# Summing part of the prompt's expert rows with ScalarE and the Pool, in a fused diffusion backbone step

## The reference, cut to what matters

```python
gate = jax.nn.softmax(best_s, axis=-1).astype(hb.dtype)
act = jax.nn.gelu(jnp.einsum('thkd,td->thk', u_tab[idx], hb), approximate=False)
return jnp.einsum('thk,thkd->td', gate * act, v_tab[idx])
...
x = x + g2 * peer_ffn(hff, lp['peer_wq'], lp['peer_keys'], lp['peer_u'], lp['peer_v'])
```

## Time and profile before

| | us |
|---|---|
| median of 3 runs | 4969.91 (4968.59 to 4973.04) |
| the profiled execution | 4967.69 |
| its span, first to last instruction | 4965.9 |
| TensorE (PE) matmuls busy | 3861.3 (78%) |
| VectorE (DVE) busy | 3242.6 (65%) |
| ScalarE (ACT) busy | 748.0 (15%) |
| Pool busy | 1447.9 (29%) |
| slot matmuls, line 680, in three groups by source | 1865.1 + 687.8 |
| dots, line 1218 | 831.5 + 420.8 + 312.1 |
| gathers, share of the 16 DMA engines | 67.4% |
| mean granted TensorE clock | 0.929 |

### The profile page before, as it was taken

How to read it: one execution, slowest core, us unless ns; L and a number is a source line. 1 busy time by engine, 2 the same in 40 slices (tenths; PEclk the granted TensorE clock), 3 DMA queues, 4 the chain that set the end, 5 groups by cost and what they waited for, 6 DMA issues and landing times. The chain is left out here.

```text
span 4965.9 us, 36487 instructions
## 1 busy us (share of the span) xinstructions
PE 3861.3 (78%) x11046; PEld 1898.0 (38%) x11046; DVE 3242.6 (65%) x8263; ACT 748.0 (15%) x2211; POOL 1447.9 (29%) x1284
## 2 busy tenths in 40 slices
PE   7588678988777776788868786788977687777776
PEld 6464334643222222235535443346422222222222
DVE  1546765536887868854574766664378787687666
ACT  0111124211101010010121112341010100100101
POOL 0001112212454434432222021221044354354432
PEclk9788788999999999999989897899999999999999
DMA  8334456754998999999969254566389899899998
GB/s 266 99 116 178 153 188 242 252 194 192 412 415 368 421 374 414 421 390 387 365 245 366 97 203 146 206 253 220 127 354 421 365 419 421 362 421 421 407 421 341
DMA packets 342149, 1497.72 MB, mean 302 GB/s; under 512 B 31424, under 2 KB 176448, under 8 KB 178112
## 3 DMA queue, kind: packets, MB, share of 16 engines
q0 software_dynamic: 184320, 1342.26, 67.4%
q1 hardware_dynamic: 157632, 153.13, 9.6%
HBM read 1491.97 MB, written 3.31 MB: 301 GB/s over the span
## 5 line engine op out<-in xcount | busy, mean ns | idle before, releaser
L680 PE MATMUL expert_acc<-uv_ring,diag 128*128 128x512 f32 x3744 | 1865.1, 631 | 417.9 <-DVE diag L1227 407.8
L634 POOL DMA_INDIRECT uv_ring<-uv,expert_index x936 | 1050.2, 1122 | 2717.1 <-PE expert_acc L680 2174.4
L680 PEld LDWEIGHTS expert_acc<-uv_ring,diag 128*128 128x128 f32 x3744 | 688.1, 198 | 1487.8 <-DVE diag L1227 898.5
L1218 DVE CUSTOM_DVE_ANT_0 uv_ring<-uv_ring,arena 128x1024 f32<-128x1024 f32 x680 | 831.5, 1223 | 243.2 <-DMA uv_ring<-uv,expert_index 240.5
L680 PE MATMUL expert_acc<-arena,diag 128*128 128x512 f32 x1376 | 687.8, 632 | 264.2 <-DVE diag L1227 196.3
L951 ACT ACTIVATE gelu<-u_dot 128x1 f32<-128x1 f32 x1280 | 256.0, 203 | 2943.8 <-DVE u_dot L1218 2943.2
L1227 DVE TENSOR_SCALAR diag<-const_mats,expert_gate,gelu 128x128 f32<-128x128 f32 x1280 | 465.7, 364 | 308.8 <-ACT gelu L951 214.1
L634 POOL DMA_INDIRECT arena<-uv,expert_index x344 | 397.6, 1156 | 757.2 <-PE expert_acc L680 460.3
L1218 DVE CUSTOM_DVE_ANT_0 arena<-arena 128x1024 f32<-128x1024 f32 x344 | 420.8, 1223 | 172.6 <-DMA arena<-uv,expert_index 171.2
L680 PEld LDWEIGHTS expert_acc<-arena,diag 128*128 128x128 f32 x1376 | 243.4, 195 | 698.1 <-DVE diag L1227 425.2
L1218 DVE CUSTOM_DVE_ANT_0 uv_ring<-uv_ring,prompt_rows 128x1024 f32<-128x1024 f32 x256 | 312.1, 1219 | 113.4 <-DMA uv_ring<-uv,expert_index 112.9
(11 more groups left out here) (202 smaller groups left out, 2785.0 us busy)
## 6 DMA issues: line engine op xcount, KB each, us to landing
w_ring<-w_ada SPq DMA_DIRECT2D x66, 512.0 KB, 11.3
w_ring<-w_in SPq DMA_DIRECT2D x64, 512.0 KB, 5.0
w_ring<-w_pq SPq DMA_DIRECT2D x64, 512.0 KB, 4.5
w_ring<-w_out SPq DMA_DIRECT2D x32, 512.0 KB, 6.3
uv_ring<-w_ada SPq DMA_DIRECT2D x30, 512.0 KB, 5.3
uv_ring<-uv,expert_index POOLq DMA_INDIRECT x936, 11.7
arena<-b_ada SPq DMA_DIRECT2D x48, 128.0 KB, 6.2
arena<-uv,expert_index POOLq DMA_INDIRECT x344, 15.7
```

The lines of the kernel that those rows point to most:

```text
L634: pool.indirect_dma_start(out=UV[j], out_offset=None, in_=uv, in_offset=bass.IndirectOffsetOnAxis(ap=idxs[:, n % 2, k:k + 1], axis=0)).the ...
L680: ins = pe.matmul(acc[:, half, :], diag[:, m % DIAGS, :], UV[SLOT_AT[m]][:, D + 512 * half:D + 512 * half + 512], start=(k == 0), stop=(k ...
L1218: V_.tensor_tensor_reduce(UV[j][:, 0:D], UV[j][:, 0:D], rows_of(n), 1.0, 0.0, ALU.mult, ALU.add, dots[:, m % DOTS:m % DOTS + 1]).then_inc( ...
```

## The change

In blocks 0 and 5, slots 84 to 127 take another path. VectorE's dot and ScalarE's gelu stay. ScalarE then multiplies gate and gelu (128x1) and multiplies the gathered v by it in place (128x1024). The Pool clears a 1024-column tile once per block and adds each weighted row to it, in its own queue between the gathers: before it issues the gather that reuses a buffer, it adds the row that lies there. VectorE builds no diag and TensorE issues no matmuls for these 44 slots. At m = 130 TensorE waits for the Pool's last add and adds its sum to `expert_acc` with two matmuls by the identity (`fold`); add_peer waits for that.

The table's rows change too: attention's steps advance by 1 each (24, m = 60 to 83), the output stage's by 2 and 1 in turn (24, m = 84 to 107), the second norm's by 3 as before, the sixteen query tiles by 1 each (m = 111 to 126). Four advances (m = 127 to 130) are left for `rest()`.

The diff, cut to its core; left out are the new buffer and semaphores, and four places where a wait for all sums of a block becomes `all_summed`:

```diff
@@ -142,7 +142,7 @@
 BESIDE_SAMPLE = points(("n1", [7], 2), ("pa", range(4), 2), ("pa", range(4, 8), 1), ("px", range(6), 1),
                        ("pg", range(4), 1), ("conv", [5], 4), ("taps", range(4, 30, 5), 2), ("cT", [3], 4), ("st", range(8), 3), ("yT", [3], 3), ("v", [4], 3), 
-                       ("head", range(0, 24, 2), 2), ("head", range(1, 24, 2), 1), ("wo", range(16), 1), ("n2", [7], 3), ("pq", range(8), 2))
+                       ("head", range(24), 1), ("wo", range(0, 16, 2), 2), ("wo", range(1, 16, 2), 1), ("n2", [7], 3), ("pq", range(16), 1))
 BESIDE_PROMPT = points(("mod", range(24), 2), ("n1", [1], 3), ("pa", range(2), 2), ("pz", range(2), 2), ("px", range(6), 1),
                        ("pg", range(4), 1), ("conv", [5], 2), ("taps", range(4, 30, 5), 1), ("cT", [0], 2), ("st", range(2), 3),
@@ -172,6 +172,29 @@
 SLOT_AT, SLOT_BEFORE, SLOT_TURN = slot_buffers()
+POOL_FROM = 84
+def by_pool(n, k):
+    return n % NBLK == 0 and k >= POOL_FROM
+def sums_before(n, k):
+    slots = [by_pool(m // SLOTS, m % SLOTS) for m in range(n * SLOTS + k)]
+    return slots.count(False), slots.count(True)
+PE_SLOTS = [m for m in range(L * NBLK * SLOTS) if not by_pool(m // SLOTS, m % SLOTS)]
+POOL_SLOTS = [m for m in range(L * NBLK * SLOTS) if by_pool(m // SLOTS, m % SLOTS)]
+TURN = {m: i for of in (PE_SLOTS, POOL_SLOTS) for i, m in enumerate(of)}
+FOLD_AFTER = {n: SLOTS + 2 for n in range(L * NBLK) if any(by_pool(n, k) for k in range(SLOTS))}
+FOLDS = sorted(FOLD_AFTER)
 class Beside:
...
@@ -426,6 +450,10 @@
         gsum = at(13568, 2, PH)
         htok = [at(13584, D), at(ARENA - 512 - D, D)]
         psum_out = at(ARENA - 512, 512)
+        def pool_sum(n):
+            return htok[1] if n % NBLK == 0 else htok_p[:]
         w_loaded = [ctx.enter_context(nc.semaphore(f"w_loaded{k}")) for k in range(NW + AHEAD)]
...
@@ -500,6 +531,20 @@
         def blk(l, g, b):
             return l * NBLK + FIRST_BLOCK[g] + b
+        def summed(eng, m):
+            if by_pool(m // SLOTS, m % SLOTS):
+                eng.wait_ge(s_pa, TURN[m] + 1)
+            else:
+                eng.wait_ge(s_vs, TURN[m] + 1)
+        def all_summed(eng, n):
+            pe_slots, pool_slots = sums_before(n, 0)
+            eng.wait_ge(s_vs, pe_slots)
+            if pool_slots:
+                eng.wait_ge(s_pa, pool_slots)
         def w_unit(l, g, kind, u):
...
@@ -616,13 +661,33 @@
         @block.gpsimd
         def _(pool):
+            def add_row(m, first):
+                n = m // SLOTS
+                if first:
+                    if n % NBLK == 0:
+                        pool.wait_ge(*s_sup.at(n // NBLK, 1, 7))
+                    else:
+                        pool.wait_ge(s_pup.sem, n)
+                    nc.gpsimd.memset(pool_sum(n), 0.0).then_inc(pool_chain, 1)
+                    pool.wait_ge(pool_chain, FOLDS.index(n) + 1)
+                else:
+                    pool.wait_ge(s_pa, TURN[m])
+                pool.wait_ge(s_pw, TURN[m] + 1)
+                nc.gpsimd.tensor_tensor(pool_sum(n), UV[SLOT_AT[m]][:, D:2 * D], pool_sum(n), ALU.add).then_inc(s_pa, 1)
             for l in range(L):
                 for g in range(2):
                     for b in range(GROUP_BLOCKS[g]):
                         n = blk(l, g, b)
+                        mine = [n * SLOTS + k for k in range(SLOTS) if by_pool(n, k)]
+                        added = 0
                         for k in range(SLOTS):
                             m = n * SLOTS + k
                             j = SLOT_AT[m]
+                            while added < len(mine) and mine[added] <= SLOT_BEFORE[m]:
+                                add_row(mine[added], added == 0)
+                                added += 1
                             if k == 0:
                                 pool.wait_ge(*s_idx.at(l, g, 2 * b))
                                 if g:
@@ -630,9 +695,11 @@
                             elif g and k == SLOTS // 2:
                                 pool.wait_ge(*s_idx.at(l, g, 2 * b + 1))
                             if SLOT_BEFORE[m] >= 0:
-                                pool.wait_ge(s_vs, SLOT_BEFORE[m] + 1)
+                                summed(pool, SLOT_BEFORE[m])
                             pool.indirect_dma_start(out=UV[j], out_offset=None, in_=uv,
                                                     in_offset=bass.IndirectOffsetOnAxis(ap=idxs[:, n % 2, k:k + 1], axis=0)).then_inc(s_gat[j], 16)
+                        for i in range(added, len(mine)):
+                            add_row(mine[i], i == 0)
         @block.tensor
@@ -675,15 +742,25 @@
                 m = n * SLOTS + k
                 if n and k == 0:
                     pe.wait_ge(s_pup.sem, n)
-                pe.wait_ge(s_dg, m + 1)
+                pe.wait_ge(s_dg, TURN[m] + 1)
                 for half in range(2):
-                    ins = pe.matmul(acc[:, half, :], diag[:, m % DIAGS, :], UV[SLOT_AT[m]][:, D + 512 * half:D + 512 * half + 512],
+                    ins = pe.matmul(acc[:, half, :], diag[:, TURN[m] % DIAGS, :], UV[SLOT_AT[m]][:, D + 512 * half:D + 512 * half + 512],
                                     start=(k == 0), stop=(k == SLOTS - 1), skip_group_check=True)
                 ins.then_inc(s_vs, 1)
+            def fold(n):
+                pe.wait_ge(s_pa, sums_before(n + 1, 0)[1])
+                for half in range(2):
+                    ins = pe.matmul(acc[:, half, :], C[:, C_ID, :], pool_sum(n)[:, 512 * half:512 * half + 512],
+                                    start=False, stop=(FOLD_AFTER[n] > SLOTS), skip_group_check=True)
+                ins.then_inc(s_fold, 1)
             def add_beside(n, m):
-                if 2 <= m <= SLOTS + 1:
+                if 2 <= m <= SLOTS + 1 and not by_pool(n, m - 2):
                     add_v(n, m - 2)
+                if m == FOLD_AFTER.get(n):
+                    fold(n)
             beside = Beside(add_beside)
@@ -950,9 +1027,20 @@
                 act.wait_ge(s_dot, m + 1)
                 nc.scalar.activation(gel[:, m % DOTS:m % DOTS + 1], dots[:, m % DOTS:m % DOTS + 1], ACT.Gelu).then_inc(s_gel, 1)
+            def weigh(n, k):
+                m = n * SLOTS + k
+                act.wait_ge(s_gel, m + 1)
+                chain(nc.scalar.activation(weight[:, m % DOTS:m % DOTS + 1], gel[:, m % DOTS:m % DOTS + 1], ACT.Copy,
+                                           scale=gat[:, n % 2, k:k + 1]))
+                v = UV[SLOT_AT[m]][:, D:2 * D]
+                nc.scalar.activation(v, v, ACT.Copy, scale=weight[:, m % DOTS:m % DOTS + 1]).then_inc(s_pw, 1)
             def gelu_beside(n, m):
                 if m < SLOTS:
                     gelu(n, m)
+                    if by_pool(n, m):
+                        weigh(n, m)
             beside = Beside(gelu_beside)
...
@@ -1221,17 +1309,19 @@
             def weigh(n, k):
                 m = n * SLOTS + k
-                if m >= DIAGS:
-                    dve.wait_ge(s_vs, m - DIAGS + 1)
+                if TURN[m] >= DIAGS:
+                    dve.wait_ge(s_vs, TURN[m] - DIAGS + 1)
                 dve.wait_ge(s_gel, m + 1)
-                V_.tensor_scalar(diag[:, m % DIAGS, :], C[:, C_ID, :], gat[:, n % 2, k:k + 1], gel[:, m % DOTS:m % DOTS + 1],
+                V_.tensor_scalar(diag[:, TURN[m] % DIAGS, :], C[:, C_ID, :], gat[:, n % 2, k:k + 1], gel[:, m % DOTS:m % DOTS + 1],
                                  ALU.mult, ALU.mult).then_inc(s_dg, 1)
             def add_peer(n):
                 g = 1 if n % NBLK else 0
                 tmp = psum_out if g else htok_p[:, 0:512]
-                dve.wait_ge(s_vs, (n + 1) * SLOTS)
+                all_summed(dve, n + 1)
+                if n in FOLDS:
+                    dve.wait_ge(s_fold, FOLDS.index(n) + 1)
                 for k in range(2):
                     x = X[:, n % NBLK, 512 * k:512 * k + 512]
                     chain(V_.tensor_tensor(tmp, acc[:, k, :], G[:, gate_tile(n // NBLK, 1, g), 512 * k:512 * k + 512], ALU.mult))
@@ -1243,7 +1333,7 @@
             def dot_beside(n, m):
                 if m < SLOTS:
                     dot(n, m)
-                if 1 <= m <= SLOTS:
+                if 1 <= m <= SLOTS and not by_pool(n, m - 1):
                     weigh(n, m - 1)
                 if m == SLOTS + 2:
                     add_peer(n)
```

More of the change, by code:

```diff
@@ L326, in build @@
         gel = sb("gelu", [P, DOTS])
+        weight = sb("expert_weight", [P, DOTS])
         diag = sb("diag", [P, DIAGS, P])
@@ L480, in build @@
         s_dg = ctx.enter_context(nc.semaphore("diag_ready"))
+        s_pw = ctx.enter_context(nc.semaphore("v_weighted"))
+        s_pa = ctx.enter_context(nc.semaphore("v_added_by_pool"))
+        s_fold = ctx.enter_context(nc.semaphore("pool_sum_folded"))
         s_vs = ctx.enter_context(nc.semaphore("v_summed"))
@@ L565, in _ @@
                     elif l:
-                        sp.wait_ge(s_vs, blk(l - 1, 1, 3) * SLOTS)
```

(5 more changed lines are left out.)

## The result

The changed kernel takes 4939.44 us (median of 4 runs, 4936.9 to 4940.14), the kernel before 4971.48 in the same session: ratio 0.9926, interval 0.9914 to 0.9939. It is faster, as forecast, and inside the range; but by 32 us, where the forecast was 80. The profiled execution has a span of 4937.2 us against 4965.9, 28.7 less.

What follows compares the result with a forecast made beforehand. TensorE was taken to bound the output stage and query projection, and likeliest attention. Terms -17 - 1 - 5 - 25 + 8 = -40 us a layer, -80 for two, gave 4890 us (own range 4870 to 4910; whole range 4840 to 4965).

Steps and rivals of the forecast that it cites:

- Attention (-17): Attention: 36 slots become 24, the 12 removed at 1.69 us each times TensorE's share 0.85; -17 us a layer.
- Output stage (-1): Output stage: 16 slots become 24, nearly all on the Pool's path; 81.5 us against 83, -1 us a layer.
- P: Pool's time per slot in the output stage: issue 1.24, add 2.45 and 0.06, together 3.75 us.
- 10.2 + 19P: Output stage's forecast length: 10.2 us for its ends plus 19 Pool periods, 81.5 us in all.
- The rival of the turns: Pool's add and VectorE's dot exclude each other: period 4.2 us, output stage +7, total 4914; chance 0.22.
- Norm (-5): Second norm: without two slots on TensorE the projection starts 6.8 us earlier, 2 given back; -5 us, range 0 to 7.
- Projection (-25): Query projection: 15 slots' matmuls leave TensorE at 1.69 us each; -25 us a layer.
- Tail (+8): After the query projection: the last slot's weighing, add and fold delay block 1's scores; +8 us a layer, 6 to 11.
- The clock: Output stage: TensorE falls to 1.2 GHz as it has gaps; +27 us a layer, total 4944; chance 0.08.
- The quick Pool: Pool's add takes 1.225 us, output stage falls to 59 us; -64 us a layer, total 4842; chance 0.10.
- The slow Pool: Output stage: Pool's add becomes the bound; slower than before from 4.6 us an add, 4992 at 4.9; chance 0.16.

Runs made afterwards that it cites:

- e1: The kernel before with only the table of rows changed, all 44 late slots still on TensorE; ratio 1.0018, 4989.35 us.
- e3: The changed kernel with the Pool's add cut from 1024 columns to one, the rest of that sum left out; ratio 0.9764, 4868.47 us.
- e4: The changed kernel with the Pool's add replaced by a memset of 2048 columns, the same sum left out; ratio 0.9809, 4886.89 us.
- e5: The changed kernel with the gather for slot m issued after row m-4 is added instead of row m-5; ratio 0.9889, 4920.55 us.
- e7: The changed kernel with odd slots of 84 to 107 back on TensorE and each gather issued one add later; ratio 0.9878, 4908.84 us.

## Why the prediction was right, and where it failed

**Attention (-17): right, a little small.** -21.1, the whole of the 12 slots by TensorE (12 x 1.69 = 20.3). The discount for the 0.85 of TensorE's share was not needed, as far as one can tell: with the same 24 slots the stage lasts 129.5 to 135.8 us in the other traces.

**Output stage (-1): wrong, by 22 us a layer; the term P, the Pool's period.** The forecast had the issue at 1.24 us with the dot free to run beside it, which gave P = 3.75. Of the period's parts, the add was right (2.45, measured 2.36 in the median) and the issue was not: 0.27 + 1.99 instead of 1.24 + 0.06, since it starts inside a dot and is held by it. The measured mean is 4.45, so 19 x (4.45 - 3.75) = 13 us of the error are the period's. Some 6 us are the ends: from the first drain to the first add it takes 6.6 us, not 3, and from the twentieth add to the stage's end 9.7, not 7.2. The last 3 us are an error of counting: my 10.2 + 19P runs from the first drain, and I set it against the 83 us from the first matmul, where the same stretch was 79.7. By my own formula the forecast should have been +2 and not -1.

The rival of the turns named the mechanism and gave 0.22 to it, with 4.2 for P, +7 on the stage and 4914 in all. The kind was right, the size too small (+21 on the stage): for its 4.2 it let the dot fit in part beside the issue. Its sign was there too: dots of more than 1.3 us, 1401 ns in the mean. Rows that tell otherwise were in the trace of before, and I read them without pairing them. A dot and an issue beside it, twice:

```profile
885.74 1.22 DVE L1218 CUSTOM_DVE_ANT_0 uv_ring<-uv_ring,prompt_rows 128x1024 f32<-128x1024 f32 x1
...
886.08 1.69 POOL L634 DMA_INDIRECT uv_ring<-uv,expert_index  x1 [4.40 <-PE expert_acc L680]
```

```profile
1193.43 1.22 DVE L1218 CUSTOM_DVE_ANT_0 arena<-arena 128x1024 f32<-128x1024 f32 x1 [8.19 <-DMA arena<-uv,expert_index]
1193.69 1.78 POOL L634 DMA_INDIRECT uv_ring<-uv,expert_index  x1 [0.30 <-issue]
```

An issue that starts inside a dot ends at 886.08 + 1.69 - 885.74 = 2.03 us after the dot's start, and 1193.69 + 1.78 - 1193.43 = 2.04: the dot's 1.22 and then 0.82 more. That is no accident of two rows: in the trace of before, 369 issues start less than 1.00 us after a dot's start, and 360 of them end 2.02 to 2.05 us after it; the other nine, which start in its first 0.04 us, take 0.94. One that starts before the dot keeps its 0.94 (e1: 949.39 and 949.64 above). With that, the full period in turns follows: 2.35 for the add, 0.22 to the dot, 2.04, 0.02 to the next add, 4.63.

**Norm (-5): half right.** -2.1 and -0.7. The projection's first matmul does start as VectorE's last column is done (1023.25 + 10.29 below), but counted from the stage's start that is only 3.6 us earlier than before, not 6.8: one of the small operations of the row is held by the last adds, as the turns rival had it (L1279, a 128x4 operation of some 0.17 us, takes 2.93). Where nothing holds it, the stage is shorter (30.5 in e3, 29.0 in e4). Then TensorE starts at the lower clock: the granted clock of 1033.6 to 1036 us is 0.50, and the first drain comes 8.73 us after the first matmul, where it was 7.12.

```profile
1015.93 2.93 DVE L1279 TENSOR_SCALAR newton<-newton 128x4 f32<-128x4 f32 x1
1016.48 2.35 POOL L677 TENSOR_TENSOR arena<-uv_ring,arena 128x1024 f32<-128x1024 f32 x1
...
1023.25 10.29 DVE L1293 TENSOR_SCALAR hT<-rotating,modc 128x128 f32<-128x128 f32 x32 [2.39 <-PE rotating L727]
...
1033.60 11.63 PE L977 MATMUL rotating<-hT,w_ring 128*128 128x512 f32 x23 [5.50 <-DVE hT L1293]
```

**Projection (-25): right,** -24.9 in both layers, all sixteen tiles but the one with the score blocks at 6.87 us.

**Tail (+8): right,** +8.4 and +9.2, and by its steps (Copy, add, fold, transposes, gather):

```profile
1152.62 1.15 ACT L1037 ACTIVATE uv_ring<-uv_ring,expert_weight 128x1024 f32<-128x1024 f32 x1
...
1153.91 2.34 POOL L677 TENSOR_TENSOR arena<-uv_ring,arena 128x1024 f32<-128x1024 f32 x1 [0.39 <-ACT uv_ring L1037]
...
1156.31 3.57 PE L755 MATMUL expert_acc<-arena,const_mats 128*128 128x512 f32 x4 [4.77 <-POOL arena L677]
...
1159.71 1.04 PE L727 MATMUL rotating<-const_mats,hT 128*128 128x128 f32 x8
...
1165.10 0.95 POOL L699 DMA_INDIRECT arena<-uv,expert_index  x1 [8.84 <-PE rotating L968]
```

The fold takes 3.57 us, not 1.7: TensorE had idled for 4.77 us, and the granted clock of 1156 to 1160 us is 0.57, most of it the lower level of 1.2 GHz. I had given 1 us for that, and 1.9 came.

**The other rivals.** The clock: 0.83 in the output stage, as in part expected, but TensorE had 37 us to spare there. The quick Pool: no, 2.36. The slow Pool, which ends slower than before, had its threshold at a mean period of 5.9 us; the real one came to 4.45, so the sum stayed on the fast side. But the ends were longer as well: 18.6 us were gained in this layer, and over 19 periods it would have taken only 1 us more a slot, from any source, to lose them.

## What to carry to other kernels

Before moving work to the Pool, look in the trace for its instructions beside VectorE's and subtract start times: an issue whose length depends on when a dot began tells of something that the two engines share, and it will be paid once a slot. Price such a queue by its period, turns included. Place its slots where the host stage's own step is longer than that period (here the query tiles, 6.87 us), or where the step with the slot on the old path is (here a single output step, 5.17 us), and not two to a short step. And check a shift of rows with the old path by itself; here it was worth nothing.

## What the runs showed of the hardware beyond that

- A Pool add of 128x1024 float32 takes 2.36 us (2.34 at least); a memset of 2048 columns 1.82, of 1024 0.97; an add of one column 0.69 by the profile.
- A VectorE operation can be held by an add that starts after it. L1654 (0.43 us alone) at 969.56 starts 0.47 us before the add of 970.03 and is held to that add's end; so is e5's dot of 951.86, 0.46 us before the add of 952.32. Both start while the Pool's issue runs. The issue alone doesn't do it: in e5 an L1654 that starts inside a held issue (956.16), with the next add 1.5 us away, takes 0.42, and in e4 one that starts 0.44 us before the memset of 941.35, inside a held issue too, takes 0.42. The add alone doesn't do it either: in e7 an L1654 that starts at 914.56 with no issue running, 0.01 us before an add, takes 0.42, and it is the add that is longer, 2.67. Why the two together do wasn't tried.
- A dot is not held by an issue that started before it: of 552 such dots in the trace of before none takes over 1.26 us.
- ScalarE's 128x1024 Copy in place kept its 1.15 us beside all of it (1.147 to 1.156 in all 88). The output stage's matmuls average 389 ns against 379 before, at a granted clock of 0.83 against 1.00.
